# Constant products on TensorE ahead of ten waits, with the banks claimed before those waits

## What is computed

```python
mp = jnp.split(silu_ctx @ w_mod[i] + b_mod[i], N_MOD, axis=-1)
hp = modulate(xp, mp[0], mp[1])
# layer 0: input projection, depthwise conv, two-way state-space scan, spatial gating, output projection, dense SwiGLU
z, xbc, dt_raw, u, v = jnp.split(h @ w_in, [i1, i2, i3, i4], axis=-1)
# layer 1: latent attention with rotary keys (8 heads), then SwiGLU of the best 2 of 8 experts
s = jnp.einsum('bqhd,bkhd->bhqk', qi, k) * scale
top_logit, top_e = lax.top_k(logits, TOP_K)
return (jax.nn.silu(xb @ wg[e]) * (xb @ wu[e])) @ wd[e]
```

## Time and profile before

| | before |
|---|---|
| median of 3 runs, us | 1924.35 (1921.73 to 1925.68) |
| profiled execution, us | 1944.56 |
| its span, us | 1942.8 |
| mean granted TensorE clock | 0.981 |
| TensorE busy | 1843.7 us, 95% |
| VectorE, ScalarE busy | 28%, 21% |
| chain that ended last: TensorE, DMA, VectorE | 88%, 5%, 3% |
| granted clock at half, us from the start | 18.7 to 25.5; 28.9 to 35.7; 52.8 to 59.6; 431.7 to 435.1; 814.0 to 820.8; 844.7 to 848.1; 899.3 to 906.1; 998.3 to 1001.7; 1011.9 to 1015.4; 1885.7 to 1889.2; from 1919.9 to the end |

### The profile page before, as it was taken

One profiled execution on the slowest core, in us unless ns is written; L12 is line 12 of the kernel. 1 busy time (PEld: TensorE's weight loads), 2 busy tenths in 40 slices (PEclk: granted clock), 3 DMA queues, 4 the chain that ended last, 5 costly groups with the idle time before them and its releaser, 6 DMA issues.

```text
span 1942.8 us, 31565 instructions
## 1 busy us (share of the span) xinstructions
PE 1843.7 (95%) x13609; PEld 1284.4 (66%) x13609; DVE 536.8 (28%) x1168; ACT 400.4 (21%) x901; POOL 125.2 (6%) x123
## 2 busy tenths in 40 slices
PE   6999999999999999999989999999998999999994
PEld 3554655879999887554785454568653456878783
DVE  2550336135555102165352000201111111111131
ACT  2221226110001001353222110311122121212120
POOL 0000111000000000000001001110010101020202
PEclk8999999999999999999999999999999999999997
DMA  8632237246542234133266556997689998999993
GB/s 311 236 132 87 87 109 260 86 140 206 175 152 76 96 126 177 51 134 134 80 244 216 200 195 204 392 383 251 228 278 394 384 364 301 365 344 359 345 383 126
DMA packets 234141, 427.93 MB, mean 220 GB/s; under 512 B 17694, under 2 KB 88701, under 8 KB 233678
## 3 DMA queue, kind: packets, MB, share of 16 engines
q1 hardware_dynamic: 218496, 411.65, 60.1%
q0 software_dynamic: 11360, 12.43, 1.9%
q10 hardware_dynamic: 4142, 1.72, 0.3%
HBM read 427.34 MB, written 29.00 MB: 235 GB/s over the span
## 4 chain that ended last, share of the span: by engine, by line
PE 88%; DMA 5%; DVE 3%; issue 2%; SPq 1%; ACT 1%; POOL 0%; POOLq 0%; DVEq 0%; ACTq 0%
PE bank L1099 24%; PE bank L588 11%; PE bank L824 10%; PE bank L1227 6%; PE bank L1192 6%; PE bank L876 6%; PE bank L635 4%; PE bank L1130 2%; PE bank L700 2%; PE bank L494 2%; DMA ring<-in_moe_w_gate_dram 2%; DMA ring<-in_w_mod_dram 1%; PE bank L919 1%; PE bank L908 1%; PE bank L552 1%
## 5 line engine op out<-in xcount | busy, mean ns | idle before, releaser
L1099 PE MATMUL bank<-ring,HTXN 128*32 128x384 f32 (+3 forms) x3104 | 287.6, 393 | 6.0 <-issue 3.9
L1318 ACT ACTIVATE arena<-bank 128x512 f32<-128x512 f32 (+3 forms) x317 | 140.8, 507 | 588.7 <-PE bank L824 178.6
L1099 PEld LDWEIGHTS bank<-ring,HTXN 128*32 128x32 f32 (+2 forms) x3104 | 202.9, 120 | 84.1 <-issue 61.1
L1099 PE MATMUL bank<-arena,HTXN 128*32 128x384 f32 (+3 forms) x2336 | 224.4, 394 | 2.6 <-issue 1.6
L1099 PEld LDWEIGHTS bank<-arena,HTXN 128*32 128x32 f32 (+2 forms) x2336 | 157.4, 122 | 63.3 <-issue 44.8
L2274 DVE TENSOR_TENSOR arena<-arena,bank 128x512 f32<-128x512 f32 x120 | 76.7, 683 | 414.3 <-PE bank L1099 385.2
L588 PE MATMUL bank<-ring,HTXN 128*128 128x512 f32 (+4 forms) x528 | 153.0, 452 | 1.0 <-DVE HTXN L2105 1.0
L1663 ACT ACTIVATE arena<-bank 128x512 f32<-128x512 f32 x120 | 65.0, 597 | 372.8 <-PE bank L1099 325.4
L588 PEld LDWEIGHTS bank<-ring,HTXN 128*128 128x128 f32 x528 | 96.2, 190 | 57.1 <-issue 47.2
L824 PE MATMUL bank<-HTXN,arena 128*128 128x192 f32 x704 | 121.4, 326 | 0.0
L876 PE MATMUL bank<-ring,arena 128*128 128x256 f32 x528 | 114.2, 379 | 2.6 <-DVE arena L2032 2.6
(11 more groups left out here) (349 smaller groups left out, 1849.0 us busy)
## 6 DMA issues: line engine op xcount, KB each, us to landing
ring<-in_moe_w_up_dram SPq DMA_DIRECT2D x53, 1024.0 KB
ring<-in_moe_w_gate_dram SPq DMA_DIRECT2D x49, 1024.0 KB
ring<-in_w_mod_dram SPq DMA_DIRECT2D x24, 2048.0 KB, 9.3
ring<-in_moe_w_down_dram SPq DMA_DIRECT2D x48, 1024.0 KB
arena<-in_moe_w_down_dram SPq DMA_DIRECT2D x40, 1024.0 KB
arena<-in_moe_w_gate_dram SPq DMA_DIRECT2D x39, 1024.0 KB
arena<-in_moe_w_up_dram SPq DMA_DIRECT2D x35, 1024.0 KB
ring<-in_w_in_dram SPq DMA_DIRECT2D x10, 2048.0 KB, 11.6
```

Of the source, the lines that this page charges most:

```text
L1099: last = mm(bank[row:row + rows_, col:col + cn], xe[:, i, k, at:at + rows_], wt[:, c0:c0 + cn], start=(k == 0 and col == 0), stop=(k == KT ...
L1318: return act_fn(out, in_, ACT.Copy)
```

## The change

`keep_awake(bank, n)` multiplies the identity by 256 columns of constants (identity and upper triangle) n times into a bank. It is called in nine places, and a tenth piece is a loop of twelve products of 128 columns into unused columns of a bank that is already being accumulated. The bank that these write is the one that the next real work was going to claim, so the claim (`fill`) is moved ahead of the wait. In `blocks` the wait itself moves inside, behind the claim. What the constant products write is overwritten by the real ones, which start their banks afresh, or lies beside what is read. The pieces: 7 before the second block of modulation rows, 7 before the first input projection, 12 small ones before its second half, 5 before the dense layer, 5 before the turn of the compressed queries, 4 before the turn of the third tile (the second latent key tile is being expanded ahead of it), 3 before the fourth probability tile, 5 before the router's input, 3 before its logits, 3 before the ranks.

```diff
--- before.py
+++ after.py
@@ -487,9 +487,17 @@
                 last.then_inc(chunk_used, 1)
                 released[label] = (chunk_used, used[0])
 
-            def blocks(label, sources):
+            def keep_awake(bank, n):
+
+                for _ in range(n):
+                    mm(bank[:, 0:2 * P], ident, CST[:, 0:2 * P], start=True, stop=True)
+
+            def blocks(label, sources, ready=None, n=0):
 
                 bank, full = fill(label)
+                if ready is not None:
+                    keep_awake(bank, n)
+                    pe.wait_ge(*ready)
                 for k, src in enumerate(sources):
                     last = tp(bank[:, k * P:(k + 1) * P], src, ident)
                 last.then_inc(full, 1)
@@ -502,25 +510,26 @@
             tp(bank[:, 0:112], praw[0:112, 0, :], ident[0:112, 0:112])
             tp(bank[:, 112:223], praw[0:111, 1, :], ident[0:111, 0:111]).then_inc(full, 1)
 
-            def to_feature_major(n):
+            def to_feature_major(n, awake=0):
 
                 for t in range(NT):
-                    pe.wait_ge(xn_ready, NT * n + t + 1)
                     for half in range(2):
-                        blocks(("nt", n, t, half), [XN[:, t, (4 * half + k) * P:(4 * half + k + 1) * P] for k in range(4)])
+                        blocks(("nt", n, t, half), [XN[:, t, (4 * half + k) * P:(4 * half + k + 1) * P] for k in range(4)],
+                               (xn_ready, NT * n + t + 1) if half == 0 else None, awake if t == 0 else 0)
 
             def ht_ready(n):
                 for t in range(NT):
                     pe.wait_ge(*drained(("nt", n, t, 0)))
                     pe.wait_ge(*drained(("nt", n, t, 1)))
 
-            def mod_rows(layer, j, at=None):
+            def mod_rows(layer, j, at=None, n=0):
 
 
                 label = ("mod", layer, j)
+                bank, full = fill(("mr", layer, j), at)
+                keep_awake(bank, n)
                 landed(label)
                 w = part(label, KT, 512)
-                bank, full = fill(("mr", layer, j), at)
                 for k in range(KT):
                     q = 32 * (k % 4)
                     last = mm(bank[q:q + 2, :], sv[:, :, k], w[:, k, :], start=(k < 4), stop=(k >= 4))
@@ -597,16 +606,17 @@
 
             mod_rows(0, 0)
             mod_columns(0, 0)
-            mod_rows(0, 2)
+            mod_rows(0, 2, n=7)
             first_rows(0)
             mod_columns(0, 2)
+            begun = [fill(("xbc", m, "p")) for m in range(4)]
+            spare = turn[0] % BANKS
+            turn[0] += 1
+            keep_awake(begun[0][0], 7)
             for t in range(NT):
                 pe.wait_ge(*drained(("nt", 0, t, 0)))
             landed(("xbc", 0))
             w = part(("xbc", 0), KT, 512)
-            begun = [fill(("xbc", m, "p")) for m in range(4)]
-            spare = turn[0] % BANKS
-            turn[0] += 1
 
             def begin(m):
                 for k in range(4):
@@ -627,6 +637,8 @@
                 label = ("xbc", j)
                 landed(label)
                 w = part(label, KT, 512)
+                for _ in range(12 if j == 0 else 0):
+                    mm(begun[0][0][:, TOK:TOK + P], ident, CST[:, 0:P], start=False, stop=False)
                 for t in range(NT if j == 0 else 0):
                     pe.wait_ge(*drained(("nt", 0, t, 1)))
                 for m in range(4):
@@ -817,6 +829,8 @@
             for j in (10, 11):
                 mod_grouped("ffn", 0, j)
             to_feature_major(1)
+            first_plain = fill(("plain", 0))
+            keep_awake(first_plain[0], 5)
             ht_ready(1)
 
             def half_product(bank, at, a, b, first, last_):
@@ -825,7 +839,7 @@
                 return ins
 
             def plain_products(n):
-                bank, full = fill(("plain", n))
+                bank, full = first_plain if n == 0 else fill(("plain", n))
                 half_product(bank, 0, quarter_w(n, 0, 0), quarter_x(0, 0), True, False)
                 half_product(bank, HTOK, quarter_w(n, 0, 1), quarter_x(1, 0), False, True).then_inc(full, 1)
 
@@ -928,8 +942,7 @@
                 pe.wait_ge(ckv_ready, t + 1)
                 turn_ckv(t)
             for t in range(NT):
-                pe.wait_ge(qa_ready, t + 1)
-                blocks(("qaT", t), [qa[:, t, k * P:(k + 1) * P] for k in range(3)])
+                blocks(("qaT", t), [qa[:, t, k * P:(k + 1) * P] for k in range(3)], (qa_ready, t + 1), 5 if t == 0 else 0)
             for i in range(len(TILES)):
                 if i + 1 < len(TILES):
                     expand(i + 1)
@@ -937,9 +950,10 @@
                 if i == len(TILES) - 1:
                     for j in (8, 9, 10, 11):
                         mod_grouped("mla", 1, j)
-                pe.wait_ge(kq_ready, i + 1)
+                last_k = i + 1 < len(TILES) and TILES[i + 1][0] == "k" and all(kind == "q" for kind, _ in TILES[i + 2:])
                 for q in range(2):
-                    blocks(("hT", i, q), [KQN[:, i % 2, 4 * q + k, :] for k in range(4)])
+                    blocks(("hT", i, q), [KQN[:, i % 2, 4 * q + k, :] for k in range(4)],
+                           (kq_ready, i + 1) if q == 0 else None, 4 if last_k else 0)
                 blocks(("hT", i, 2), [kq_v[:, i % 2, D + k * P:D + (k + 1) * P] for k in range(4)])
 
 
@@ -973,8 +987,7 @@
             for n, (h, t) in enumerate(HEAD_TILES):
                 if n + AHEAD < len(HEAD_TILES):
                     scores(n + AHEAD)
-                pe.wait_ge(pr_ready, n + 1)
-                blocks(("pT", n), [PR[:, n % 4, k * P:(k + 1) * P] for k in range(1 if t == 0 else 3)])
+                blocks(("pT", n), [PR[:, n % 4, k * P:(k + 1) * P] for k in range(1 if t == 0 else 3)], (pr_ready, n + 1), 3 if n == 3 else 0)
                 if t == 1 and h > 0:
                     values(h - 1)
             gate_rows(1, 2, 2)
@@ -987,9 +1000,10 @@
 
             gate_rows(1, 5, 3, (0,))
             first_ahead = pe.mark_branch_hint_location()
-            to_feature_major(3)
+            to_feature_major(3, 5)
+            bank, full = fill("lg_lanes")
+            keep_awake(bank, 3)
             ht_ready(3)
-            bank, full = fill("lg_lanes")
             for k in range(KT):
                 q = 32 * (k % 4)
                 last = mm(bank[q:q + 8, 0:TOK], wrt[:, k, :], HT[:, k, :], start=(k < 4), stop=(k >= 4))
@@ -1006,8 +1020,9 @@
                 last = mm(bank[:, 8 * t:8 * t + 8], lg_lanes[:, t * P:(t + 1) * P], pick[:, 0:NE], start=True, stop=True)
             last.then_inc(full, 1)
             rows_again(1)
+            bank, full = fill("rank")
+            keep_awake(bank, 3)
             pe.wait_ge(sel_ready, 1)
-            bank, full = fill("rank")
             tiles = sel.rearrange("p t e -> p (t e)")
             mm(bank[:, 0:24], before, tiles, start=True, stop=False)
             mm(bank[:, 24:48], ones, tiles, start=False, stop=False)
```

## The result

The changed kernel took 1917.92 us (median of seven runs, 1915.48 to 1926.84) where the kernel before took 1924.87 beside it. The ratio of all the runs is 0.9969, 95% interval 0.9957 to 0.9982: a gain of 7 us by the medians and of 6 us (3.5 to 8.3) by the ratio. Ratios are of the fast runs alone, which leaves out two of the experiments' runs, of 2380 and 4682 us. The forecast was 13.7 us of gain and 1910.7 us, with a range down from 1917.6; the result lies 0.3 us outside, and the gain is half of what was forecast. The profiled execution took 1915.48 us with a span of 1913.7 and a mean granted clock of 0.992 (0.981 before). Of the nine stretches at 1.2 GHz ahead of the experts, two short ones are left in this execution, 3.4 us each from 642.4 and from 888.2 us; the first of them had no counterpart in the table of before.

The account below looks back on a forecast made before the run. TensorE was taken to bound the kernel up to the experts, with nine stretches at 1.2 GHz. 2.7 + 2.7 + 2.7 + 1.6 + 3.0 + 1.7 - 1.3 + 0.6 + 0 = 13.7 us off 1924.35: 1910.7 us, range 1905.5 to 1917.6.

Parts of the forecast that it names:

- Before each piece TensorE was at full clock in the trace: Argument against late products: the clock is full when each of the ten pieces starts, so each fits its wait.
- the term of 2.7 us: Second block of modulation rows: seven products fill a 3.56 us wait, work behind runs at full clock, 2.7 us off.
- The rival of the late products: All ten pieces: if the clock is already low, pieces outlast their waits, 16.8 us lost, 1941 us; chance 0.04.
- falls only during the wait: At each piece: the clock drops only while TensorE waits, given as a reason against late products.
- The list of stretches: Before 1020 us: nine stretches at 1.2 GHz, each beginning during or just after a TensorE wait; the terms remove their cost.
- I take the same microseconds off the median: Whole kernel: 13.7 us read from the profiled execution, 20 us slower than the median, subtracted from 1924.35 us.
- I take +1.3 us, near the middle: Fourth probability tile: three products with nothing to hide in, between +2.6 and -1.7 us, taken as 1.3 us lost.
- The partial rival: Ahead of the experts: only part of the drops goes, gain 6.8 us, time 1917.6 us; chance 0.22.
- the first three terms: Second block of modulation rows and both halves of the first input projection: 2.7 us each, 8.1 us together.
- The constants don't count: All pieces: mostly zero products don't keep the clock, all drops stay, only cost is left, 1926.9 us; chance 0.06.
- the experts take the gain back: Experts: the forecast would be wrong if they take back what the first half gained; no size given.
- the wait at the first gather: First gather: the wait on rows from memory should grow if the ranks' part got faster; no size given.

Follow-up runs that it names:

- zeros: The changed kernel with every constant product made of zeros only, weights and columns; 1917.96 us, ratio 0.9954 to the kernel before.
- warmed start: Changed kernel with four products before the rows of parameters, ten for seven in the first piece, timed with the probability piece in the next scores' bank: 1915.35 us.
- claims: The changed kernel with all constant products taken out and the claims of banks kept ahead of the waits; 1928.27 us, ratio 1.001 to the kernel before.
- before again: The kernel before, unchanged, timed and profiled once more; 1926.86 us, ratio 0.9995.
- transposes: The changed kernel with each 256-column constant product replaced by four 128-column transposes, the twelve small products kept; 1915.89 us, ratio 0.9949 to the kernel before.
- the repairs: Changed kernel with the warmed start and five products ahead of the down projection, the probability piece kept, moved or dropped; 1914.42 to 1917.38 us.
- the last pair: The changed kernel with the repairs, probability piece left in place, 1915.04 us, against the changed kernel on the same chip, 1917.63 us.

## Why the prediction was wrong

The mechanism was right: low stretches follow bare waits, products of no use to the result keep the full clock (zeros do it too), and the claims are free. Between the two profiled executions seven of the eight terms that the forecast put at other than nought came out within 0.3 us. The size failed: 13.7 us were forecast, 12.5 came between the two first traces ahead of the experts, 8.6 between the means of three, and 6 to 7 in the runs (6.0, 6.2 and 10.0 by the ratios of three timings, so the 8.6 of the traces is within their scatter). Four steps of the text are behind that:

- *"Before each piece TensorE was at full clock in the trace."* For the first piece that is a property of the execution, not of the kernel: in 8 of 14 traces without a warmed start the clock rose only at 19.9 us or later. Then the term of 2.7 us is gone (the modulation rows start at 21.5 to 23.0 us in place of 19.8), and over three traces each it measured 0.4 us. The rival of the late products was worked out for all ten pieces together and set aside by this one observation, when the case that mattered was the first piece alone. In the first trace of before the record of the granted clock begins at full only at 15.2 us, barely ahead of the place. That it "falls only during the wait" was read too quickly as well: at 844.7, 998.3 and 1011.9 us it fell behind the wait's end.
- *The list of stretches.* The sum took away what before had and asked nothing of the waits that had no stretch behind them. The wait of 2.6 us at the down projection now has one in every trace of the change (and in all eight others of kernels with some of the pieces but none at this wait; not in claims or before again), and costs 1.7 us. In one of the three a stretch at 326 us cost another 1.7, in one the stretch at 873 us cost 2.0. Why there, and why not in before, stays open.
- *"I take the same microseconds off the median."* The terms were read from one execution which was slower than the median of the runs by 20 us. It had 51.2 us at 1.2 GHz ahead of its last stretch, before again 41.0 and claims 44.4, and it reached the experts 3.9 and 1.4 us later than these: 1.8 us less to win on the mean. The rest of the excess sat in the experts, 922.4 us for 909.7 and 907.8, and had nothing to do with the terms, as the text assumed.
- *"I take +1.3 us, near the middle."* The middle of +2.6 and -1.7 is +0.45. The price of 1.3 was right against an execution without a low stretch there, but what it stood in the sum against was before's trace with one, and there the step cost 0.0, 0.0 and -1.7 us in the three traces of the change. This one error is on the careful side.

The partial rival priced a gain of 6.8 us at 1917.6 us and gave it 0.22. That the measured 1917.92 is nearly this number is luck. It was to come of the first three terms in full and nothing of the later ones, or of slow work beside transposes; in the traces the first three together gave 5.2 us for 8.1, the later ones came nearly whole, and new stretches took some of it back.

"The constants don't count" is refuted by zeros, transposes and claims. That the experts take the gain back is refuted by the windows: they take 905.8, 906.5 and 906.7 us in the three traces of the change, not more than the 907.8 and 909.7 of before. Of the steps in what would show it, the mean clock (0.992), the 5.4 us of the sixteen records and the place of the probability products came as written. The full clock from 15 us to the probabilities did not (642 us in all three traces), and the wait at the first gather shrank from 0.90 to 0.52 us in place of growing: what the ranks won went into the wait in front of the experts' first product. The terms also aren't proportional to the time at low clock: that fell from 41.0 and 44.4 us in before again and claims to 10.2, 13.7 and 6.8 in the change, 32 us on the average, for some 8 us.

What stays open: the effect of the probability piece's place on the time within 3 us; why TensorE was held up by issue in the experts in one execution of before; and whether the repairs together are worth the 2.6 us of the last pair.

## What to carry to other kernels

Price a recurring loss from several executions before you subtract it: which waits had a low stretch behind them changed from one execution of the same program to the next. Filler work needs the state it is to preserve: give the first filler a warm-up of its own, in idle time that nothing waits behind, and put every filler into a buffer that has long been free, not into the one whose release ends the wait (3.0 us won in the traces for 0.0 to 1.7, though the medians can't tell). When the known waits are filled, look at the bare ones that did no harm before.

## What was not expected of the hardware

- The clock's first rise isn't a fixed property of a program: in executions that reach the first modulation rows within 0.3 us of one another it came at 14.1 to 15.2 or at 19.9 to 23.7 us. With four products from 5.35 us on it came at 8.4 to 9.2 or 14.2 to 14.7 us.
- Products of zeros by zeros hold the full clock as those of the identity and the triangle do (10.2 us of low clock in both), and so do pieces of nothing but 128x128 transposes (10.2 us).
- A low stretch can stand behind a wait that had none before: new ones of 3.4 us stood at 642 to 650 us in all three traces of the change, and at about 872 us in all five of the kernels with both repairs and in one of the change.
- The same short wait is followed by a low stretch in one execution and not in another: behind a wait of 0.78 us near 324 us one of three traces of the change has it (1.7 us lost), and behind the bare wait of 1.50 us at the probabilities before has 6.8 us of it and before again none (3.1 us).
- TensorE can go through one stretch of narrow products (128x32 weights) in 12.5 or in 16.6 us in two executions, with no semaphore to blame, only "issue".
